# A sparse-attention stage put in another order: the compressed branch's source is projected first, and its steps stand between the units of the other projections

## The reference, cut to what matters

```python
kv = (h @ w_kv).reshape(B, S, 6, G, dh)          # G = 4 groups, dh = 64
k_cmp, v_cmp = rotary(kv[0], pos), kv[1]
k_slc, v_slc = rotary(kv[2], pos), kv[3]
k_win, v_win = rotary(kv[4], pos), kv[5]
def compress(t, pe, w1, w2):                     # idx: 15 windows of 32 tokens, stride 16
    flat = (t[:, :, idx, :] + pe).reshape(B, G, n_cmp, CMP_LEN * dh)      # ... x 2048
    return jax.nn.gelu(flat @ w1) @ w2           # w1 2048 x 256, w2 256 x 64
k_c, v_c = compress(k_cmp, ...), compress(v_cmp, ...)
q = rotary(x @ w_q[:, :1024]); gates = sigmoid(x @ w_q[:, 1024:])         # 16 heads
o_cmp = masked_softmax(q @ k_c) @ v_c
out = gates[0] * o_cmp + gates[1] * o_slc + gates[2] * o_win
return out @ w_out
```

## Time and profile before

| | |
|---|---|
| median of 3 runs | 2936.55 us (2936.34 to 2941.26) |
| the profiled execution's own time | 2942.53 us |
| its span | 2940.6 us |
| busy in the span: PE, DVE, ACT | 91%, 73%, 55% |
| mean granted TensorE clock | 0.956 of 2.4 GHz |
| the stage: first chunk done, last X unit done, first attention scores, attention done | 1628.5, 1682.0, 1748.4, 1820.4 us |

### The profile page before, as it was taken

One profiled execution on the slowest core, in us unless ns is written; L12 is line 12 of the kernel. 1 busy time (PEld: TensorE's weight loads), 2 busy tenths in 40 slices (PEclk: granted clock), 3 DMA queues, 4 the chain that ended last, 5 costly groups with the idle time before them and its releaser, 6 DMA issues.

```text
span 2940.6 us, 39620 instructions
## 1 busy us (share of the span) xinstructions
PE 2685.3 (91%) x12842; PEld 2171.0 (74%) x12842; DVE 2134.2 (73%) x2576; ACT 1609.4 (55%) x2090; POOL 19.8 (1%) x37
## 2 busy tenths in 40 slices
PE   3889989988989999998999968699999999999997
PEld 2767768876767787766898746577888888888875
DVE  6765567776656755855555765589899999989998
ACT  2554444445544444433444444377777777777775
POOL 0000000000000000000000000000000000000000
PEclk9999999998999999999999968799999999999998
DMA  6655458755545554644555420499999999999995
GB/s 231 223 151 165 157 179 264 250 186 166 171 143 165 188 192 158 222 129 138 165 181 162 135 83 10 154 312 362 335 339 359 333 365 330 357 342 332 368 353 205
DMA packets 357958, 665.96 MB, mean 226 GB/s; under 512 B 23009, under 2 KB 57313, under 8 KB 357201
## 3 DMA queue, kind: packets, MB, share of 16 engines
q1 hardware_dynamic: 354080, 648.51, 65.3%
q0 software_dynamic: 3760, 15.91, 1.6%
HBM read 663.29 MB, written 1.05 MB: 226 GB/s over the span
## 4 chain that ended last, share of the span: by engine, by line
PE 80%; DVE 8%; ACT 5%; issue 2%; DVEq 2%; DMA 2%; ACTq 0%; SPq 0%
PE ps L445 44%; PE ps L451 21%; PE ps L465 2%; DVE wlo L1788 2%; PE ps L556 2%; ACT whi L1272 1%; PE ps L470 1%; DVE mod_sum L1812 1%; PE ps L1175 1%; DMA raw<-in_w_ada 1%; PE ps L655 1%; DMA ada_raw<-in_w_ada 1%; ACT att L1492 1%; PE ps L767 0%; DVEq L1811 0%
## 5 line engine op out<-in xcount | busy, mean ns | idle before, releaser
L1788 DVE TENSOR_TENSOR wlo<-raw,whi 128x1024 fp32r<-128x1024 f32 x709 | 864.2, 1224 | 478.0 <-ACT whi L1272 468.7
L1272 ACT ACTIVATE whi<-raw 128x1024 fp32r<-128x1024 f32 x709 | 746.7, 1059 | 741.3 <-PE ps L451 636.0
L445 PE MATMUL ps<-whi,xh 128*128 128x512 f32 (+2 forms) x1248 | 457.3, 376 | 13.4 <-issue 9.4
L445 PE MATMUL ps<-whi,xl 128*128 128x512 f32 (+2 forms) x1248 | 445.2, 367 | 0.0
L445 PE MATMUL ps<-whi,gathered_hi 128*128 128x512 f32 x896 | 361.8, 404 | 3.3 <-DVE att L2062 2.6
L445 PE MATMUL ps<-whi,gathered_lo 128*128 128x512 f32 x896 | 355.2, 396 | 0.0
L451 PE MATMUL ps<-wlo,xh 128*128 128x512 f32 (+2 forms) x1248 | 294.5, 363 | 0.0
L445 PEld LDWEIGHTS ps<-whi,xh 128*128 128x128 f32 x1248 | 241.4, 193 | 57.4 <-issue 15.2
L451 PE MATMUL ps<-wlo,gathered_hi 128*128 128x512 f32 x896 | 282.7, 396 | 0.0
L445 PEld LDWEIGHTS ps<-whi,xl 128*128 128x128 f32 x1248 | 241.4, 193 | 37.6 <-issue 1.9
L445 PE MATMUL ps<-whi,yh 128*128 128x512 f32 (+2 forms) x592 | 241.1, 409 | 13.4 <-DVEq L1904 6.8
(11 more groups left out here) (388 smaller groups left out, 3595.4 us busy)
## 6 DMA issues: line engine op xcount, KB each, us to landing
raw<-in_moe_w_in SPq DMA_DIRECT2D x227, 512.0 KB, 5.4
spare<-in_moe_w_in SPq DMA_DIRECT2D x165, 512.0 KB, 5.7
mod_b<-in_moe_w_out SPq DMA_DIRECT2D x165, 512.0 KB, 5.5
raw<-in_w_ff SPq DMA_DIRECT2D x128, 512.0 KB, 4.6
raw<-in_w_in SPq DMA_DIRECT2D x96, 512.0 KB, 3.7
work<-in_moe_w_in SPq DMA_DIRECT2D x56, 512.0 KB, 5.5
work<-in_moe_w_out SPq DMA_DIRECT2D x56, 512.0 KB, 5.2
raw<-in_w_ada SPq DMA_DIRECT2D x48, 512.0 KB, 4.7
```

The costliest lines, as they stand in the source:

```text
L445: e.matmul(ps[0:lhs[2], banks[t], at:at + width], part[:, k0 + j, t * P:t * P + lhs[2]], whi[:, slot, w], start=first and j == 0 and part ...
L1272: e.activation(whi[:, slot, :], src, ACT.Copy).then_inc(split_hi, 1)
L1788: e.tensor_tensor(wlo[:, slot, :], src, whi[:, slot, :].bitcast(F32), ALU.subtract).then_inc(split_lo, 1)
```

## The change: what it does

Unit 0 is kv0.0. `at(i, ...)` puts a step at position i: on PE behind unit i, on ACT and DVE behind the split of unit i + 3. PE:

```diff
+                at(5, block_turns(1))
+                at(6, block_turns(0))
+                at(12, source)
+                at(17, own_query_turns(0))
+                at(23, own_query_turns(4))
+                at(32, own_key_turns(0))
+                at(37, own_key_turns(1), hidden_turns)
+                at(39, cmp_heads)
...
+                        if name == "v" and i == 0:
+                            source(e)
+                        unit(e, (flat_h[w], flat_l[w], CW), 1, i * UROWS, (4 + w,), CMP_HID, i == 0, i == 7)
...
             def own_attention(e):
-                source(e)
-                clear(e)
-                for kind in range(2):
...
-                clear(e)
-                cmp_scores(e)
+                chunks_read(e)
+                e.wait_ge(job_act, c.at("job_a"))
+                e.wait_ge(job_dve, c.at("job_d"))
                 for i in range(NSA_STEPS + 2):
                     if i < NSA_STEPS:
                         own_scores(e, i)
+                    if i == 0:
+                        clear(e)
+                        cmp_scores(e)
```

ACT (it also makes the value half of the double copy, `twice_values`, which DVE made before):

```diff
+                at(4, twice_values)
+                at(6, lambda e: jobs(e, [shift_copy(1, 0), None]))
+                at(7, lambda e: jobs(e, [shift_copy(0, 0), None]))
+                at(8, rounded(1))
+                at(9, rounded(0))
+                at(18, heads(4))
+                at(21, gelu(1))
+                at(24, heads(6))
+                at(33, heads(0))
+                at(36, gelu(0))
+                at(38, heads(2), lambda e: jobs(e, hidden_heads(plain)))
```

DVE, where a rotary piece now takes both token tiles at once (six operations on 256 elements, seven pieces), and the windows are added in two operations per branch:

```diff
-                        rope_heads(e, proj[:, t, at:at + heads * HD].rearrange("p (h d) -> p h d", h=heads), heads, 32,
-                                   cos, sin, 5120)
+                        src = proj[:, :, first:first + 256].rearrange("p t (h d) -> p t h d", h=4)
+                        shape = [P, NT, 4, 32]
...
+                        rope(e, src[:, :, :, 0:32], src[:, :, :, 32:64], cos, sin, t1, t2)
+                        if tell:
+                            to_pe(e)
...
-                    for b in range(16):
-                        src = kv_shift[w][:, :, 2 * b:2 * b + CMP_STRIDE * (N_CMP - 1) + 1:CMP_STRIDE]
-                        e.tensor_scalar(flat[w][:, b, :].rearrange("p (g n) -> p g n", g=NSA_G), src,
-                                        pe_col[:, w, b:b + 1], None, ALU.add)
+                        for b in range(2):
...
+                            e.tensor_tensor(flat[w][:, 8 * b:8 * b + 8, :].rearrange("p b (g n) -> p b g n", g=NSA_G), src,
+                                            pe_col[:, w, 8 * b:8 * b + 8].rearrange("p (b o u) -> p b o u", o=1, u=1)
+                                            .broadcast_to([P, 8, NSA_G, N_CMP]), ALU.add)
...
+                at(4, rope_heads_of_tiles(0, True), twice(work, 0))
+                at(5, small_weights)
+                at(6, lambda e: jobs(e, [None, shift_copy(1, 2)]))
+                at(7, lambda e: jobs(e, [None, shift_copy(0, 2)]), windows(1))
+                at(8, windows(0))
+                at(9, remainder(1))
+                at(10, remainder(0))
+                at(12, rope_heads_of_tiles(1536, True))
+                at(15, rope_heads_of_tiles(1792, tell=True))
+                at(18, heads(4), rope_heads_of_tiles(2048, True))
+                at(21, rope_heads_of_tiles(2304, tell=True))
+                at(24, heads(6))
+                at(29, rope_heads_of_tiles(512, True))
+                at(30, twice(key_twice[0], 512))
+                at(33, heads(0))
+                at(34, rope_heads_of_tiles(1024, True))
+                at(35, twice(key_twice[1], 1024))
+                at(38, heads(2), lambda e: jobs(e, [None, value_heads]))
```

More of the change, by code:

```diff
@@ L334, in program @@
         key_ready = sem("key_ready")
+        hid_ready = sem("hid_ready")
         out_hi, out_lo = sem("out_hi"), sem("out_lo")
@@ L1096, in sparse_attention @@
[L1096 to L1105, removed]
@@ L1121, in values @@
-                def values(e, bank):
-                    for s in range(2):
-                        for b in range(2):
-                            mm = e.matmul(ps[0:CH, bank, s * HD:(s + 1) * HD], cmp_hid_heads[:, b, s * CH:(s + 1) * CH],
-                                          cmp_w2[:, 1, b, :], start=b == 0, stop=b == 1)
-                    return mm
-                job(e, keys)
-                job(e, values)
-                clear(e)
+                base, X = c.n.get("unit", 0), (xh, xl, P)
@@ new lines, in src, with at, block_turns, piece @@
+                def src(t, b):
+                    return x[:, t, b * P:(b + 1) * P]
+                def at(i, *pieces):
+                    c.weave.setdefault(base + i, []).extend(pieces)
+                def block_turns(w):
+                    def piece(e):
+                        if w:
+                            c.add("key", NT)
+                            e.wait_ge(key_ready, c.at("key"))
+                        else:
+                            source(e)
+                        for g in range(0, NSA_G, 2):
+                            def fill(e, bank):
+                                for j in range(2):
+                                    for t in range(NT):
+                                        at = w * 512 + (g + j) * P
+                                        tr = e.transpose(ps[:, bank, (j * NT + t) * P:(j * NT + t + 1) * P],
+                                                         work[:, t, at:at + P], ident)
+                                return tr
+                            side_job(e, fill)
+                    return piece
@@ L2487, in sparse_attention, with at, rope_heads_of_tiles @@
             def sparse_attention(e):
-                def rope_piece(t, at, heads, wait=False):
+                base = c.n.get("unit", 0)
+                def at(i, *pieces):
+                    c.weave.setdefault(base + i, []).extend(pieces)
+                def rope_heads_of_tiles(first, wait=False, tell=False):
                     def piece(e):
@@ L2547, in values, with remainder, piece, heads @@
+                def remainder(w):
+                    def piece(e):
+                        from_act(e)
+                        e.tensor_tensor(flat_l[w], flat[w], flat_h[w].bitcast(F32), ALU.subtract)
+                        to_pe(e)
+                    return piece
+                def heads(n):
+                    return lambda e: jobs(e, own_head_turns(plain)[n:n + 2])
                 def values(e, bank):
```

264 lines of the change are left out of this document (151 added, 113 removed).

## The result

| | before | after |
|---|---|---|
| median of 4 runs | 2938.91 us (2936.34 to 2944.50) | 2920.57 us (2919.76 to 2921.60) |
| profiled execution, its span | 2942.53, 2940.6 us | 2919.76, 2917.9 us |
| mean granted TensorE clock | 0.956 | 0.962 |

The ratio is 0.9935, interval 0.9920 to 0.9950: 19 us less, where 24.8 were forecast. The direction held, and so did the range of 17 to 32 us of gain; the size did not quite. The forecast alone would be a ratio of 1 - 24.8/2938.91 = 0.9916, just outside the interval. As an absolute time the median lies 1.1 us above the range's end of 2919.5, which was counted from a median of 2936.55 for the kernel before. Ratios are of fast runs alone, without one execution of the kernel before, timed beside the last runs, that took 10441 us at a granted clock of 0.588.

What follows compares the result with a forecast made beforehand. Before the attention it saw a chain with no engine full, and after the change DVE as bound (78.3 us against PE's 69.5). Gains 23.5 + 1.3 = 24.8 us, from 2936.55 to 2911.7 us; range 2904.5 to 2919.5.

Steps and rivals of the forecast that it cites:

- The walk: From unit 4's start to the first attention scores, PE meeting DVE at named places: 92.7 us, 23.5 us gained.
- the price of a rotary piece: In DVE's load from unit 4 on: six operations on 256 elements, 2.5 us a piece, seven pieces 17.5 us.
- the wait before `v.0`: PE ahead of the first value unit, waiting for the first window remainder: 1.5 us.
- The first query wait: PE ahead of the first query transposes, waiting for DVE until 34.7 us behind unit 4's start: 3.1 us.
- The stride: Window additions reading every 16th fp32 element on DVE: 0 to 1.5 us extra in all, 0.5 taken.
- The first scores ahead of the compressed ones: Compressed scores moved behind the first attention step's: gain between 0 and 3.75 us, 1.3 taken.
- The clock pays: Rival: PE stays at 1.2 GHz after waits for five more X units, 11.5 us back, 2923.3 us; chance 0.17.
- the two gate units behind the last key transposes: Near the end of the stretch to the first scores, taken at PE's low clock: 2.56 us each.
- DVE never waits: Rival: from unit 4 to the scores all hand-overs are hidden, gain 35.0 + 1.3 us, 2900.2 us; chance 0.14.
- slower: Rival: PE stays at 1.2 GHz through the interleaved section and bounds it, 10.5 us slower, 2947 us; chance 0.04.
- It does not reach the end: Rival: the expert stage takes the gain back, waiting for its weights as before, 2936 us; chance 0.03.

Runs made afterwards that it cites:

- again_timed: The changed kernel, unedited, timed again on the chip of the later runs: 2924.90 us, ratio 0.9948 to the kernel before.
- again: The changed kernel run once more without an edit, for a second profile: 2922.34 us.
- later_turns: The changed kernel with the two query transposes and their copies two units later: 2921.75 us, ratio 0.9932 to the kernel before.
- cmp_first: The changed kernel with the compressed scores again ahead of the first attention step, as in the kernel before: 2929.28 us.
- windows_unit: The changed kernel with window additions reading neighbouring elements instead of every sixteenth, so the windows hold other elements: 2925.72 us.
- better_nopad: The changed kernel with later query transposes, first value units one unit later, last keys' rotation behind their last projection unit: 2923.42 us, ratio 0.9943 to the kernel before.
- pad16: The changed kernel with 16 empty DVE drains at the start of DVE's program: 2929.78 us in one run.
- pad50: The changed kernel with 50 empty DVE drains at the start of DVE's program: 2920.91 us in one run.
- pad50_timed: The changed kernel with 50 empty DVE drains at its start, timed several times: 2917.71 us, ratio 0.9927 to the kernel before.

## Why the prediction was right, and where its size was off

**The walk** was right to 0.6 us at each of its points and to 0.3 at its end. DVE bounds the section (89% busy up to the hidden transposes), meets PE at the places named, and the price of a rotary piece was near enough. Of the parts, the wait before `v.0` was 0.7 us longer, by the stride. The first query wait came out 1.3 shorter, and that is a lesson on the wait and not on DVE: the X unit behind `v.1` ran at the low clock (4.29 us instead of 2.79), PE came later by that much, and the transposes still started when DVE was ready. In `again_timed` that unit was fast, and the wait was the 3.10 that were forecast.

**The stride** was mis-sized. The old operations of 60 elements gave 0 to 0.05 us apiece, and 0.5 us in all was taken; it is 1.4. The rule of the Trainium skill, "SBUF — State Buffer", in its note on cachelines, that elements on separate lines each pay, agrees with the 1006 ns against 655. Its place in the sum, ahead of `v.0`, was right.

**The first scores ahead of the compressed ones**: 1.3 us taken, 0.7 between the two first profiles, and some 1.0 plus a shorter wait against the reversed order at nearly the same clock (0.83 and 0.82). It held within its bounds.

**"The clock pays"** had 0.17 and did not come. After the wait of 3.10 us one X unit took 4.55 us (1673.32 to 1677.87), where 4.0 was assumed, and the next 2.79; behind the wait of 2.16 us one took 4.29 (from 1646.43), which the walk did not have. Together they cost 3.2 us over the 2.8 of a fast one, against the 11.5 of this rival, and the 1.5 of the second were hidden in PE's next wait for DVE. The warning of the Trainium skill, "TensorE: Matmul & The Clock Gate", on dense matmuls between waits, fits these two of the sixteen X units, and the two gate units behind the last key transposes (2.58 and 2.56 us), which the walk had at the low clock. **DVE never waits** and **slower** did not come either.

**"It does not reach the end"**: the ground given against this rival is the step that failed in part. The prediction wrote that the expert stage "shifts as a whole" and that all later stages are "as long as before", because no weights are loaded for it ahead of time. That reason holds: its DMA share is 0.94 before and after. But it looked only at data. Of a changed program the instructions move too, and in this one the loop of the expert stage then had instructions fetched at each return to its start, with DVE standing still for 4.5 to 5.9 us at each, at the price of 7.4 to 10.7 us (the excess of the two distances over 127.3) in every profile where the ten packets show (after, `again`, `again_timed`, `later_turns`, `cmp_first`, `windows_unit`, `better_nopad`, `pad16`) and of nothing in the six others. So the place of the instructions, which the sum does not have at all, was the missing term: 24.8 less about 8 is 17, near the 19 and the 15 (2938.9 x 0.0052) that the two sets of runs give.

**What stays open.** Which property of the place decides is not settled: fifty more instructions or 34 fewer put it right, sixteen more did not, and no run looks for the two edges. The first return costs 3.2 to 6.1 us and the second 3.6 to 6.2, in identical programs too; the gap of DVE itself is 4.5 to 5.9, and most of its spread is in how late behind the branch the packet starts, but what sets that isn't known. q14 is not DVE's queue alone: of its 30 packets of `again` between 1 and 1600 us, `pad50`, where only DVE's program moved, has 17 at the same time to 5 us and 13 elsewhere, while q8 keeps 47 of 48. That the packet ends the gap is argued from its time, and no run holds it back. No run parts the new order from the shorter work of DVE (rotary pieces and windows in fewer operations) in the 23.8 us; the walk has both. And of the 3 us that still part `pad50_timed` (21.5) from the forecast none can be told from its interval.

## What to carry to other kernels

Price a stage by a walk along the engine that will bound it, with each hand-over at its place; that held here to a fraction of a microsecond. Then compare stage by stage, not span by span: after a change that alters an engine's count of instructions, look in the untouched loops for idle time put down to "issue" and at the packets of the instruction queues, and if they grew, try some empty instructions ahead. One profile of each kernel cannot judge 3 us where the clock's phases alone move a stage by 6.

## What the runs showed of the hardware

- An untouched loop gained two waits of DVE of 3.7 to 5.0 us ahead of its first tensor operation, at its two returns, with ten more instruction packets of some 8 KB (0.08 MB by ten), only by where DVE's instructions lie: with 79 or 95 of them fewer ahead of it than at first, and not with 0, 45 or 129 fewer.
- At such a return DVE did nothing for 4.5 to 5.9 us behind its branch, in 16 of 16, with one packet of q14 starting 2.7 to 4.1 us into it; at the returns of the six other profiles it went on within 0.3 us, and so it did where the short loops inside that loop went back, in all fourteen. The four other packets of a round came with no such wait.
- An fp32 addition of 480 elements per partition on DVE took 655 ns at unit stride and 1006 ns at a stride of 16 elements, 0.7 ns more per element.
- The same program goes through the same stage at different granted clocks: the last 32 products of the attention took 3.68 us in one profile of the kernel before and 6.93 in the next, and the attention as a whole 77.8 and 83.6 us.
